# A three-layer transformer forward pass: the last block's tokens sorted by residue modulo 4, its attention heads two and four at a time

## The reference, cut to what matters

```python
for l in range(DEPTH_2):                              # one layer
    h = _rmsnorm(x, norm_gain[l])
    z = h @ w_in[l]                                   # 1024 x 8192
    a_in, a_gate, q, k, v, b_gp, g_logits = jnp.split(z, splits, axis=-1)
    y_a = (_multiscale_pool(a_in, ...) * jax.nn.silu(a_gate)) @ w_proj_a[l]
    att = _dilated_attention(q, k, v, rel_bias)       # 3 groups of 8 heads of 64
    y_b = (att * jax.nn.silu(b_gp)) @ w_proj_b[l]
    gates = jax.nn.sigmoid(g_logits.reshape(B, S, 2, D) + b_gate[l])
    merged = gates[:, :, 0] * y_a + gates[:, :, 1] * y_b
    x = x + merged @ w_out[l]
return _rmsnorm(x, final_gain)
```

## Time and profile before

| | |
|---|---|
| median of three runs | 1447.19 us |
| the profiled execution, its own time | 1448.71 us |
| its span, first to last instruction | 1446.9 us |
| PE busy | 1402.4 us (97%) |
| DVE, ACT, POOL busy | 815.4, 685.0, 115.0 us |
| b2, from the first transposes of t = 1 to the end | 1112 to 1447 us |

### The profile page before, as it was taken

How to read it: one execution, slowest core, us unless ns; L and a number is a source line. 1 busy time by engine, 2 the same in 40 slices (tenths; PEclk the granted TensorE clock), 3 DMA queues, 4 the chain that set the end, 5 groups by cost and what they waited for, 6 DMA issues and landing times.

```text
span 1446.9 us, 18265 instructions
## 1 busy us (share of the span) xinstructions
PE 1402.4 (97%) x6741; PEld 1146.5 (79%) x6741; DVE 815.4 (56%) x1144; ACT 685.0 (47%) x961; POOL 115.0 (8%) x166
## 2 busy tenths in 40 slices
PE   8999999899999999999999999999999999999897
PEld 6888778788888887888888788888887877777685
DVE  6655458756555556555455574555556455545554
ACT  6444345726444356444444545444446444444532
POOL 2000013400000000000004100000001000000500
PEclk9999999999999999999999999999999999999899
DMA  9655445225565544565644522655545744433430
GB/s 308 199 178 191 160 141 171 69 66 169 179 188 188 206 164 155 183 193 177 203 131 161 174 67 92 199 186 190 205 150 173 268 149 140 140 112 97 148 116 29
DMA packets 146593, 232.14 MB, mean 160 GB/s; under 512 B 8839, under 2 KB 102183, under 8 KB 146272
## 3 DMA queue, kind: packets, MB, share of 16 engines
q1 hardware_dynamic: 143648, 222.52, 46.7%
q0 software_dynamic: 2560, 8.58, 2.2%
q10 hardware_dynamic: 320, 0.16, 0.1%
HBM read 230.13 MB, written 1.10 MB: 160 GB/s over the span
## 4 chain that ended last, share of the span: by engine, by line
PE 87%; DVE 6%; ACT 3%; POOL 2%; issue 1%; DMA 0%; SPq 0%; POOLq 0%; DVEq 0%; ACTq 0%
PE acc L503 16%; PE acc L505 16%; PE acc L504 16%; PE acc L533 9%; PE acc L534 9%; PE acc L537 9%; PE misc L562 5%; PE misc L731 2%; PE misc L700 2%; DVE wl L1378 1%; PE misc L684 1%; ACT xh L1009 1%; ACT wh L973 1%; DVE xl L1404 1%; PE acc L708 1%
## 5 line engine op out<-in xcount | busy, mean ns | idle before, releaser
L1378 DVE TENSOR_TENSOR wl<-raw,wh 128x2048 fp32r<-128x2048 f32 (+2 forms) x206 | 466.5, 2269 | 279.3 <-ACT wh L973 279.0
L973 ACT ACTIVATE wh<-raw 128x2048 fp32r<-128x2048 f32 (+2 forms) x206 | 387.5, 1888 | 161.0 <-PE acc L537 154.5
L503 PE MATMUL acc<-wh,xh 128*128 128x512 f32 (+2 forms) x1104 | 437.5, 396 | 8.7 <-DVE xl L1404 4.7
L505 PE MATMUL acc<-wh,xl 128*128 128x512 f32 (+2 forms) x1104 | 429.0, 389 | 0.0
L504 PE MATMUL acc<-wl,xh 128*128 128x512 f32 (+2 forms) x1104 | 428.4, 388 | 0.0
L503 PEld LDWEIGHTS acc<-wh,xh 128*128 128x128 f32 x1104 | 209.2, 190 | 53.4 <-issue 7.0
L505 PEld LDWEIGHTS acc<-wh,xl 128*128 128x128 f32 x1104 | 208.8, 189 | 43.1
L504 PEld LDWEIGHTS acc<-wl,xh 128*128 128x128 f32 x1104 | 209.3, 190 | 40.2 <-issue 0.5
L533 PE MATMUL acc<-wh,ah 128*128 128x512 f32 x352 | 139.4, 396 | 2.0 <-DVE a_n L1489 2.0
L534 PE MATMUL acc<-wl,ah 128*128 128x512 f32 x352 | 137.9, 392 | 0.0
L537 PE MATMUL acc<-wh,al 128*128 128x512 f32 x352 | 109.1, 391 | 0.0
(11 more groups left out here) (274 smaller groups left out, 1443.2 us busy)
## 6 DMA issues: line engine op xcount, KB each, us to landing
raw<-in_ffn_w_in_dram SPq DMA_DIRECT2D x172, 512.0 KB, 4.7
raw<-in_ffn_w_out_dram SPq DMA_DIRECT2D x88, 512.0 KB, 4.4
raw<-in_w_in_dram SPq DMA_DIRECT2D x64, 512.0 KB, 4.7
raw<-in_fox_w_in_dram SPq DMA_DIRECT2D x24, 512.0 KB, 4.2
raw<-in_ple_w_gate_dram SPq DMA_DIRECT2D x16, 512.0 KB, 4.0
win<-bias_by_offset POOLq DMA_DIRECT2D x24, 192.0 KB, 3.4
raw<-in_mla_w_o_dram SPq DMA_DIRECT2D x8, 512.0 KB, 4.0
raw<-in_fox_w_o_dram SPq DMA_DIRECT2D x8, 512.0 KB, 4.5
```

The costliest lines, as they stand in the source:

```text
L503: pe.matmul(dst, hi, rhs_h, start=first, stop=False)
L505: return pe.matmul(dst, lo, rhs_h, start=False, stop=last)
L973: act.activation(wh[:, s, 0:n], raw[:, s, 0:n], ACT.Copy).then_inc(hi_done, 1)
L1378: dve.tensor_tensor(wl[:, s, 0:n], raw[:, s, 0:n], wh[:, s, 0:n].bitcast(F32), ALU.subtract)\
```

## The change

- The tokens of b2 are sorted by residue modulo 4 (64 tokens of each). The transposed features are written in that order (`x_cols`, `turned`) into own buffers `zh`, `zl`. Each 128 sorted tokens hold tokens of both halves t, so the first fill needs both halves from its first matmul.
- `rstd` and `h` are needed in the sorted order too: POOL writes them to memory and reads them back permuted; the output is written back in the old order by four DMAs instead of two.
- Groups 1 and 2 now stay inside 128 x 128 diagonal blocks. The attention is done in 8 units: 4 of two heads (group 0), 2 of four heads (group 1), 2 of four heads (group 2). q and k of two heads are transposed together ([128 x 128]), the two heads lie in partitions 0 to 63 and 64 to 127, and their scores go to two banks ("lanes"), alternating. One half-step stands after each of the groups 6 to 23.
- The bias table is made in runs of 128, and each run is repeated 64 times in memory by nine DMAs from memory to memory (POOL, at the start of FFN f1). A unit's bias is read from it with 8 DMAs (group 0) or 4 (groups 1, 2) in pieces of 256 bytes, instead of one DMA of 1536-byte pieces per head.
- `flip` goes; with it `B2_PERM` and the reversing turn of the result. `a_in` comes first among the chunks; YAT is turned after chunk 12 instead of 13; `combine` stands after group 24 instead of 26.
- The silu of `b_gp` no longer goes ahead of attention work, that of `a_gate` stands ahead of the last unit's exponentials.
- `wide_first`: an FFN's first wide group runs its first fill for both halves, then its second.
- In `next_norm` (where one split is asked for) and in the embedding stage, the split for t = 1 comes behind `rest`.

```diff
+RES, RUN = 4, 64
+UNITS = [(0, n) for n in range(4)] + [(1, n) for n in range(2)] + [(2, n) for n in range(2)]
+NU = len(UNITS)
+U_FIRST = 6
+B2_COMBINE = U_FIRST + 2 * NU + 2
...
+            def wide_first(g, q, ah_, al_):
+
+                s = g % RING
+                for n in range(2):
+                    for t in range(NT):
+                        open_tile(q + n, t)
+                        for k in range(2):
...
+            def even(i):
+
+                if i < NU:
...
+                    heads_ = [2 * n] if grp == 0 else [4 * n, 4 * n + 2]
+                    for b in range(2):
+                        open_m(b, r[b] + 2 * i)
+                        for m, head in enumerate(heads_):
+                            for t in range(NT):
+                                o = (2 * m + t) * P
+                                mm = turn(b, slice(o, o + P), qkv_of(b, grp, t, head, P))
+                        mm.then_inc(m_ready[b], 1)
+                if i:
+                    j = i - 1
+                    for lane in range(2):
+                        pe.wait_ge(exp_done, 2 * j + lane + 1)
+                        open_m(2 + lane, r[2 + lane] + (2 - lane) * j)
+                        for m in range(4):
+                            mm = turn(2 + lane, slice(m * P, m * P + P), pr2[:, lane, m * P:m * P + P])
...
+            def odd(i):
+
...
+                    n, w = (2, S) if grp == 0 else (4, P)
+                    for m in range(n):
+                        for lane in range(2):
+                            rows = slice(HD * lane, HD * lane + HD)
+                            kc = slice(0, S) if grp == 0 else slice(m * P, m * P + P)
+                            mm = pe.matmul(M[:, lane, m * w:m * w + w], qT2[rows, m * P:m * P + P], kT2[rows, kc],
+                                           start=True, stop=True)
...
+            def attend(w):
+
+                i = (w - U_FIRST) // 2
+                if 0 <= i <= NU:
+                    (odd if (w - U_FIRST) % 2 else even)(i)
...
                 if c == 0:
-                    first_fill("n8", 8, g, q)
-                    continue
-                open_acc(q + B2_FILL[c])
+                    rows_ready(pe, 8, 1)
+                    turn_rows("n8", 1)
+                    ready = x_wait("n8")
...
-            turn_fill(q + B2_YBT, orev, True)
+            turn_fill(q + B2_YBT, orev)
...
                     residual(q, g, scale, t)
-                    if t:
+                    if t and more == 2:
                         split_to(done[0] + more)
                     rest(name, r, t)
+                if more == 1:
+                    split_to(done[0] + more)
...
                 embed(1)
+                rest(after, r + 1, 1)
                 split_to(done[0] + 1)
-                rest(after, r + 1, 1)
...
+            for j in range(NRUN):
+                pool.dma_start(scratch[:, j, :, :], bass.AP(compact, 128 * j, [[TAB, H8], [0, RUN], [1, 128]]))\
+                    .then_inc(table_wide, 16)
...
+            pool.wait_ge(rstd_done, NT * 9)
+            pool.dma_start(bass.AP(rstd_d, 0, [[1, P], [P, NT]]), rstd[:, :],
...
+                pool.dma_start(h[RUN * n:RUN * n + RUN, :, :],
+                               bass.AP(h_d, n * D, [[RES * D, RUN], [2 * D, NT], [1, D]])).then_inc(hp_in, 16)
```

More of the change, by code:

```diff
@@ L114 @@
             for n in ("mla", "fox")}
[L115 removed]
+B2_END = tuple(HEADS["b2"][1][b] + U_FILLS[b] for b in range(4))
 def fox_fill(c):
@@ L645, in ffn @@
                     pe.wait_ge(m_read[c % 2], r0[c % 2] + c // 2 + 1)
[L646 to L651, removed]
+                    if c == 0:
+                        wide_first(g, q, ah, al)
+                    else:
+                        for t in range(NT):
+                            wide_tile(g + c, q, t, ah, al, 2 * c, False, c == FCH - 1,
+                                      turn_h(after, r_after) if t and c == FCH - 1 else None)
                     if c == 0:
@@ L666, in ffn, with heads @@
                         open_m(3, r0[3] + j)
-                        pe.matmul(M[0:H8, 3, :], rb[:, H8 * j:H8 * j + H8], onehot[:, 512 * j:512 * j + 512],
-                                  start=True, stop=True).then_inc(m_ready[3], 1)
-            def heads(name, nh, dk, q_of, k_of, v_of, qkT_, pr, pT_, ready, after, full=False):
+                        for n in range(2 if j == 2 else 1):
+                            h0, c0, w = ((0, 0, 448), (0, 448, 448), (H8 * (1 + n), 896 + 128 * n, 128))[j]
+                            mm = pe.matmul(M[0:H8, 3, 128 * n:128 * n + w], rb[:, h0:h0 + H8], onehot[:, c0:c0 + w],
+                                           start=True, stop=True)
+                        mm.then_inc(m_ready[3], 1)
+            def heads(name, nh, dk, q_of, k_of, v_of, qkT_, pr, pT_, ready):
                 base = HEADS[name][1]
-                sq = PLAN[name][1] + S_FILL.get(name, 0)
+                sq = PLAN[name][1] + S_FILL[name]
                 def step(i):
@@ L679, in step @@
                         ready(i)
-                        tb, tn = (0, i) if full else (i % 2, i // 2)
+                        tb, tn = i % 2, i // 2
                         open_m(tb, base[tb] + 2 * tn)
                         for t in range(NT):
[L683 to L687, removed]
+                            turn(tb, slice(t * P, (t + 1) * P), q_of(i, t), dk)
                         for t in range(NT):
@@ L868, in _ @@
-            step = heads("b2", NH2, HD, lambda i, t: qkv_of(0, i, t), lambda i, t: qkv_of(1, i, t),
-                         lambda i, t: qkv_of(2, i, t), qkT2, pr2, pT2, b2_ready, lambda j: None, full=True)
-            def turn_fill(fill, rows, back=False):
+                    heads_ = [2 * n] if grp == 0 else [4 * n, 4 * n + 2]
+                    for b in range(2):
+                        open_m(b, r[b] + 2 * i)
+                        for m, head in enumerate(heads_):
+                            for t in range(NT):
+                                o = (2 * m + t) * P
+                                mm = turn(b, slice(o, o + P), qkv_of(b, grp, t, head, P))
+                        mm.then_inc(m_ready[b], 1)
@@ L892, in _ @@
                     wait_group(g + w)
-                    tall_group(g + w, q + B2_FILL[c], xh, xl, 4 * k, 4, 512, k == 0, k == 1)
-                    for _ in range(B2_STEPS[w]):
-                        step(at)
-                        at += 1
+                    tall_group(g + w, q + B2_FILL[c], zh, zl, 4 * k, 4, 512, k == 0, k == 1,
+                               ready if c == 0 else None)
+                    attend(w)
                 if c == 10:
@@ L1292, in _ @@
                     split_to(g + w + 3)
-                    gates_first = k == 1 and what in ("a_gate", "b_gp")
-                    if not gates_first:
-                        for _ in range(B2_STEPS[w]):
-                            b2_step(at)
-                            at += 1
+                    silus_first = k == 1 and what == "a_gate"
+                    if not silus_first:
+                        attend(w)
                     if w == B2_COMBINE:
```

461 lines of the change are left out of this document (275 added, 186 removed).

## The result

The changed kernel takes 1400.95 us (median of 4 runs, 1400.12 to 1402.41); beside it the kernel before took 1446.62 (4 runs). The ratio is 0.968, with a 95% interval of 0.967 to 0.970. The forecast was 1397.5 in a range of 1388 to 1412. The profiled execution took 1400.12 us (span 1398.3) against a sum of 1399.0.

What follows compares the result with a forecast made beforehand. PE was taken as the bound, busy for 97% of the span; -37.3 - 4.4 - 6.5 - 7.0 + 1.1 + 6.2 - 2.8 + 1.0 = -49.7 us gave 1397.5 us, with an 8 in 10 range of 1388 to 1412.

Steps and rivals of the forecast that it cites:

- step 1: Attention in b2: units take 44.4 us instead of 81.7, gaining 37.3; overlap of the two lanes' scores gains 4.4 more.
- the bound of 8.9: Attention scores in b2: at most each pair of lane matmuls takes the time of one, gaining 8.9 us.
- The rule of the Trainium skill: Attention scores: matmuls in distinct row groups run concurrently, so the whole 8.9 us would be won, giving 1393.1.
- steps 2, 3: End of b2: waits for last exponentials and POOL's sum of the groups, and both reversals, go; gains 6.5 and 7.0 us.
- The gates' wait: Late in b2: the wait for a chunk's gates moves to chunk 12 and recurs at chunk 14, costing 1.1 us.
- step 4: Start of b2: PE idles 5.1 us for `h`, then runs at half clock; cost 6.2 us, 4.0 if the clock holds.
- Cost nothing: Start of b2: the sorted `rstd`'s round trip through memory, at some 3 us a leg, delays PE by nothing.
- 5 us if each leg took 6 or more: Start of b2: upper bound for the cost of the `rstd` round trip, up to about 5 us with slow legs.
- some 45 us shorter: Sign expected in the profile: b2 from its first product to the end gets some 45 us shorter.
- step 5: FFNs and first embedding stage: waits for `a_n`, 2.0 us, and one `xl` wait, 0.8 us, go; gain 2.8.
- step 6: Transfers: copies within memory, `h` out and back, bias DMAs and output cost 1.0 us in all, bounds 0 and 8.
- the rival of late tables: Attention bias in b2: fetches of 40 us hold up DVE, 60 us lost, 1457 us; chance 0.04.

Runs made afterwards that it cites:

- experiment 2: Changed kernel with score matmuls ordered lane by lane: 1402.31 us; with both lanes' score matmuls reading rows 0 to 63, so no opposite halves: 1406.38 us.
- experiment 4: Changed kernel with the first wide group of the four FFNs going by token tile again, as before the change: 1401.45 us, ratio 0.969.
- experiment 5: Changed kernel with DVE's next split again ahead of the rests of the second token tile in the two embedding stages: 1402.24 us, ratio 0.971.

## Why the prediction was right, and where it was wrong

- **The pieces of the attention** (step 1) were right in kind. Forecast 44.4 us without overlap, found 36.3: 7.0 by overlap, 2.2 by cheaper passes in long runs, less 1.1 since a pass of 64 columns took 0.12 us instead of 0.105 while transposes were a little cheaper.
- **The overlap** (step 1) was the wrong choice between its bounds. I halved the bound of 8.9 because "a lane's second pass can only meet the other lane's first". The trace of before bore out neither end; experiment 2 shows 7.0 us by its own rows. The rule of the Trainium skill that the prediction cites was the better guide.
- **Last exponentials and sum of the groups** (steps 2, 3) hit within 0.1 us, slack of 9 us included. The gates' wait was expected to move and be met twice, at 1.1 us more; it vanished, 1.05 less. No run isolates why.
- **The start of b2** (step 4) was right in its mechanism: 5.0 us idle, the clock at 0.50, transposes in 1.65 us. It came out 1.5 us dearer. The half clock was taken to last 5.4 us from the first transpose on (2.7 of them in products); it lasted 7, and its 11 slow products cost 2.2 us, not 1.3. The 168 products with `zh` from the slow address are another 1.0; transposes, copy and rest ahead of the first product were 0.3 cheaper. "Cost nothing" for the round trip stood on "some 3 us a leg". The write took 9.8, so the trip ended at 1132 us, not 1127 to 1130. The bound "5 us if each leg took 6 or more" covered it; 0.7 us were paid, with the crowded weight transfers in the same chain, and 2.1 of what a better start would win are swallowed. The sign "some 45 us shorter" for b2 doesn't fit "from its first product": from the end of the embedding to the end it is 47.4 us, from b2's first product, which starts 6.3 us later, 54.9.
- **FFNs and first embedding stage** (step 5): 2.0 us in experiment 4 and 1.5 at the first embedding stage in experiment 5, against 2.0 and 0.8 forecast; the second was undervalued. The table shows only -1.2 because the products with `ah` got slower by 12 ns or so for each of 352 triples, about 4 us. Some 1.7 us of small gains that make up the difference are not isolated by any run.
- **Transfers** (step 6): no PE wait stands behind the nine copies, and DVE never waits for `win`, so the rival of late tables fell. Pieces from the table have no high price of their own: eight DMAs of 64 KB for a later unit were issued in 5.0 us from 1168 us on and landed in 3.1 each. In the crowded stretch at the start of b2 they took 14.1, and the weights beside them came late. That crowding was foreseen only as a sum of 1.0 us for all transfers; its part of the 0.7 us above is not separated. The output, put at 0.1 to 0.2, cost 1.1: four DMAs of 256 KB landed in 3.1 us, two of 512 KB in 2.6, and two more had to be issued.
- **The missing term**: the address of the stationary features, about 4 us up to 1107 and, with `zh` at 17 ns more for each of 288 triples than `xh` had, about 5 us in b2. Every product's price was carried over from the trace of before. A change of the memory plan moves that price, and the diff showed it (`flip` out, `rstdp` in).

## What to carry to other kernels

When a change touches a memory plan, compare the start of every stationary operand before and after (here 128 modulo 512 bytes was fast and 64, 96 and 192 were not), and the mean duration of the same products in both traces: here 32 bytes were worth 12.8 us. Put independent matmuls with 64-row operands into opposite halves of the array and alternate them, at least every second one. Before removing an idle stretch, look for what is late next; here it was a 1 KB write, and the weight transfers behind it.

## What the runs showed of the hardware that was not expected

- Products of 128 x 512 whose stationary tile starts at 128 modulo 512 bytes follow each other at 227 ns on average; at 96 or 192 modulo 512 at 233, at 64 at 229. Other starts were not run.
- Matmuls with 64 rows in opposite halves overlap almost fully at 256 columns (8 passes in 1.06 us, alone 1.92) and at 128 (16 in 1.09, alone 1.98); with four of one half ahead of four of the other two fifths of that gain are left (1.64), with two ahead of two all of it (1.07). Each matmul shows as two passes, and no row here separates which pass meets which.
- A write of 1 KB in pieces of 4 bytes took 9.2 to 10.6 us in the eleven traces that have it, beside a read back of 0.5 KB in 2.2 to 2.8 (5.0 in one).
- The same 64 KB read in pieces of 256 bytes landed in 14.1 us beside weights, `h` and `bands`, and in 3.1 and 2.6 us for the next two units that were fetched.
